# HGRN scores of levels 0 to 5: four products of 32 keys per block of 128 tokens instead of one of 128 keys

## The reference

```
q, fp, i_in, gate = split(h @ w_in, 4)
f = lb + (1 - lb) * sigmoid(fp);  k = (1 - lb) * sigmoid(-fp)
scores[t, s] = sum_k q[t, k] * k[s, k] * exp(bcum[t, k] - bcum[s, k])   for s <= t
o[t] = sum_s scores[t, s] * v[s] + (q[t] * exp(bcum[t])) @ S
S_t = diag(f_t) S_{t-1} + k_t v_t^T
```

## Time and profile before

| | us |
|---|---|
| median of 3 runs | 1762.22 |
| lowest and highest | 1761.44, 1766.76 |
| the profiled execution | 1766.25 |
| its span on the core | 1764.4 |
| mean granted TensorE clock | 0.986 |
| PE busy | 1686.6 (96%) |
| DVE busy | 1039.5 (59%) |
| ACT, POOL busy | 555.5 (31%), 382.6 (22%) |

### The profile page before, as it was taken

One profiled execution on the slowest core, in us unless ns is written; L12 is line 12 of the kernel. 1 busy time (PEld: TensorE's weight loads), 2 busy tenths in 40 slices (PEclk: granted clock), 3 DMA queues, 4 the chain that ended last, 5 costly groups with the idle time before them and its releaser, 6 DMA issues.

```text
span 1764.4 us, 27067 instructions
## 1 busy us (share of the span) xinstructions
PE 1686.6 (96%) x10586; PEld 1479.8 (84%) x10586; DVE 1039.5 (59%) x1635; ACT 555.5 (31%) x1000; POOL 382.6 (22%) x345
## 2 busy tenths in 40 slices
PE   7999999999999999999999899988999999989998
PEld 5999999989998899799998788766887887668876
DVE  5757475644765557465574345667444757764445
ACT  4323132333143232324323143544112225351121
POOL 0000000000421124041331304325341043253410
PEclk9999999999999999999999899999999999999999
DMA  3233232213221221212122123222233242212331
GB/s 125 96 93 94 66 97 85 96 48 101 72 61 60 73 70 58 82 56 72 49 73 84 48 75 104 72 72 67 77 103 113 82 140 72 72 48 82 109 119 48
DMA packets 112608, 141.95 MB, mean 80 GB/s; under 512 B 3068, under 2 KB 88480, under 8 KB 112480
## 3 DMA queue, kind: packets, MB, share of 16 engines
q1 hardware_dynamic: 108368, 133.07, 23.8%
q10 hardware_dynamic: 4032, 6.89, 1.2%
q0 software_dynamic: 80, 0.20, 0.0%
HBM read 137.01 MB, written 2.10 MB: 79 GB/s over the span
## 4 chain that ended last, share of the span: by engine, by line
PE 84%; DVE 8%; ACT 5%; issue 2%; DMA 0%; POOL 0%; SPq 0%; DVEq 0%; ACTq 0%; POOLq 0%
PE acc L363 23%; PE acc L365 23%; PE acc L364 22%; PE aux L514 5%; DVE sm L1828 1%; PE aux L363 1%; PE aux L365 1%; PE aux L364 1%; PE aux L531 1%; ACT pr L1373 1%; PE aux L422 1%; PE aux L539 1%; PE aux L541 1%; PE aux L503 1%; PE aux L1053 1%
## 5 line engine op out<-in xcount | busy, mean ns | idle before, releaser
L363 PE MATMUL acc<-xhi,whi 128*128 128x264 f32 (+2 forms) x1888 | 632.1, 335 | 10.5 <-issue 3.7
L364 PE MATMUL acc<-xlo,whi 128*128 128x264 f32 (+2 forms) x1888 | 618.3, 327 | 0.0
L365 PE MATMUL acc<-xhi,wlo 128*128 128x264 f32 (+2 forms) x1888 | 617.9, 327 | 0.0
L363 PEld LDWEIGHTS acc<-xhi,whi 128*128 128x128 f32 x1888 | 357.9, 190 | 46.9 <-issue 12.2
L365 PEld LDWEIGHTS acc<-xhi,wlo 128*128 128x128 f32 x1888 | 358.0, 190 | 30.7
L364 PEld LDWEIGHTS acc<-xlo,whi 128*128 128x128 f32 x1888 | 358.3, 190 | 27.5
L358 POOL TENSOR_TENSOR wlo<-raw,whi 128x1024 fp32r<-128x1024 f32 x84 | 205.0, 2441 | 352.5 <-DVE whi L1883 352.5
L354 ACT ACTIVATE whi<-raw 128x1024 fp32r<-128x1024 f32 x160 | 165.8, 1048 | 173.1 <-PE acc L365 157.7
L1676 DVE TENSOR_TENSOR wlo<-raw,whi 128x1024 fp32r<-128x1024 f32 x77 | 93.9, 1222 | 69.1 <-ACT whi L354 69.1
L358 DVE TENSOR_TENSOR wlo<-raw,whi 128x1024 fp32r<-128x1024 f32 x83 | 101.0, 1221 | 42.5 <-ACT whi L354 42.5
L1883 DVE CAST whi<-raw 128x1024 fp32r<-128x1024 f32 x84 | 65.7, 784 | 73.0 <-PE acc L365 73.0
(11 more groups left out here) (281 smaller groups left out, 2733.5 us busy)
## 6 DMA issues: line engine op xcount, KB each, us to landing
raw<-in_w_in SPq DMA_DIRECT2D x38, 1024.0 KB, 5.1
raw<-in_hgrn_w_in SPq DMA_DIRECT2D x32, 1024.0 KB, 5.8
raw<-in_pool_w_in SPq DMA_DIRECT2D x16, 1024.0 KB, 5.5
raw<-in_pool_w_out SPq DMA_DIRECT2D x8, 1024.0 KB, 4.9
raw<-in_hgrn_w_out SPq DMA_DIRECT2D x8, 1024.0 KB, 4.9
raw<-in_w_out SPq DMA_DIRECT2D x8, 1024.0 KB, 4.9
raw<-in_pool_w_grp SPq DMA_DIRECT2D x4, 1024.0 KB, 5.5
raw<-in_w_branch_attn SPq DMA_DIRECT2D x4, 1024.0 KB, 4.9
```

Of the source, the lines that this page charges most:

```text
L363: pe.matmul(dst, stat[0], mov[0], start=first, stop=False)
L364: pe.matmul(dst, stat[0], mov[1], start=False, stop=False)
L365: return pe.matmul(dst, stat[1], mov[0], start=False, stop=last)
```

## The change

At levels 0 to 5 each block of 128 tokens gets four products of 32 keys on the diagonal: keys 32n to 32n + 31 by the same 32 tokens' queries (level 0), or by their 16 queries in second halves (levels 1 to 5), written to partitions 32n to 32n + 31. The masked copies are the same and read all 128 partitions; what is off the diagonal is masked away there, and `aux` is set to zero once, on DVE, ahead of the HGRN stage.

```
-                    for c in range(CH if level <= MASKED else 0):
-                        keys = kb[par][x][:, META + P * c:META + P * c + P]
-                        q = qb[par][x][:, P * c:P * c + P]
+                    for c, n in [(c, n) for c in range(CH) for n in range(4)] if level <= MASKED else []:
+                        rows = slice(32 * n, 32 * n + 32)
+                        keys = kb[par][x][:, META + P * c + 32 * n:META + P * c + 32 * n + 32]
+                        q = qb[par][x][:, P * c + 32 * n:P * c + 32 * n + 32]
                         if level == 0:
-                            dst = small[:, P * c:P * c + P]
+                            dst = small[rows, P * c + 32 * n:P * c + 32 * n + 32]
                         else:
                             q = second_halves(q, m)
-                            dst = small[:, 64 * c:64 * c + 64].rearrange("p (b m) -> p b m", m=m)
+                            dst = small[rows, 64 * c + 16 * n:64 * c + 16 * n + 16]
+                            dst = dst.rearrange("p (b m) -> p b m", m=m)
                         mm = pe.matmul(dst, keys, q, start=True, stop=True)
...
             weighted_inverse(dve, 1)
+            dve.memset(aux[:, :, :], 0.0)
```

## The result

| | us |
|---|---|
| the kernel before, median of 4 runs | 1761.83 (1760.91 to 1766.76) |
| the changed kernel, median of 4 runs | 1732.44 (1731.22 to 1733.81) |
| ratio | 0.9828, 95% interval 0.9808 to 0.9848 |
| the changed kernel, profiled execution | 1731.74, span 1729.9 |

The change makes the kernel 29.4 us faster. 1728.5 was forecast, in a range of 1719 to 1748.

A forecast was written before the change was run, and what follows sets the result against it. PE was taken to bound the kernel; 41.8 us from cheaper steps, less 7.0 of waiting for DVE and 1.1 of memset, gave 33.7 us, so 1728.5 us against the median of 1762.22, range 1719 to 1748.

The forecast's parts named there:

- PE bounds the stage: HGRN stage: PE is busy for 96% of the span, so every us it saves counts until another engine is late.
- the step cost 1.79 us before: One level of both heads on PE, levels 0 to 5: 1.79 us each, 48 steps, 86 us.
- A changed step costs what level 6 costs: Levels 0 to 5 on PE: 0.84 us written out, 1.00 in the loop, four bands overlapping; gain 41.8 us.
- the straight line: PE's time per record extrapolated from 128 keys (107 ns) and 64 keys (67 ns): 47 ns at 32 keys.
- slower: Rival: neighbouring bands don't overlap, each small record takes 47 ns; 62 us more, 1825 us; chance 0.04.
- two readings: Level steps: four bands overlap, or rival, they give no more than two: 16.7 us gain, 1745.5 us, chance 0.22.
- The memset has no cover: Zeroing `aux` on DVE ahead of PE's third HGRN unit: its whole length goes onto PE, 1.1 us.
- What is late next: PE waits for DVE's level work at levels 2 and 3: 1.0 us a pair in 7 pairs, 7.0 us given back.
- POOL at nothing: POOL's level work, 3.46 us in its densest window, was costed at nothing.
- The sum 41.8 - 7.0 - 1.1 = 33.7: Whole kernel: PE's gain from cheaper steps, less waiting for DVE, less the memset, in us.
- DVE takes more: Rival: DVE's stretch of levels 1 to 4 sets the pace, 2.2 us a pair; 25.3 us gain, 1737; chance 0.12.

The follow-up runs named there:

- the one, two and four bands: Changed kernel with all products written to one band or two bands, against its own four: steps of 2.016, 1.009 and 0.554 us first to last start.
- e1: Changed kernel with DVE's queue reordered: factors of the pair to come and weight split placed behind level work; 1721.61 us, ratio to before 0.9751.
- e2: Changed kernel with level 1 alone put back to one product of 128 keys by 64 queries per block; 1732.41 us.

## Why the prediction was right, and which term was off

- **PE bounds the stage, and the step cost 1.79 us before.** Right: 91.5 us over 42 steps include what the unit itself takes between the same records.
- **A changed step costs what level 6 costs, since a band gets as many records.** Right, and shown by the one, two and four bands. Nearly free of waits (kernel e1) the 42 steps gained 91.5 - 55.6 = 35.9 us; the forecast for them was 24 x 0.79 + 18 x 0.95 = 36.1. The steps in the loop gained 0.80 us each, the others 0.92. Pair 7 gained 5.5, the forecast was 5.7. One price beside it was off: by the straight line a record of 32 keys on one band took 47 ns, and the rival "slower" was reckoned with that; it takes 32. The mechanism is what I read from two bands; that neighbours don't share a path was my choice between two readings, with 0.22 for the other, and no row before could tell.
- **The memset has no cover.** Right: 0.91 us of record, 0.9 us of wait, 1.1 forecast.
- **What is late next.** The engine, the cause and the first place were right (level 2, for the masked copies of L581, now L584), the size was not: this is the term that was mis-sized. I took 1.0 us a pair, 7.0; it is 64.4 - 55.6 = 8.8, and 9.7 us, 1.4 a pair, with the 0.9 at level 6, which no forecast wait covers. Its split was off as well: I had 0.6 us at level 2 and 0.3 to 0.5 at level 3, and it is 8.0 of the 8.8 us at level 2, 1.1 a pair, and 0.7 at level 3, 0.1 a pair. At level 2 I had reckoned with one wait; there are two, since each head waits for its own copy (0.46 and 0.44 us in the rows shown; over the pairs the stretch of level 2 grew from 2.25 to between 2.40 and 2.74 us, where kernel e1 has 1.33 to 1.42). I had also let DVE's rows keep their length and start, but they start with the unit's end and the two rows of factors grew from 0.55 + 1.11 to 1.00 + 0.86 us. POOL's work of level 1 starts at 442.47 now and runs beside the first of them (442.63), where it ran beside the second before (445.54 and 445.74). It is what I suspect for the growth; no run tested it.
- **What I had no row for.** In pairs 0 and 2 the last of level 6's 32 records starts 0.50 and 0.47 us behind the one before it, which is the 0.9 us of level 6; the 31 ahead of it, the second head's too, come at their usual pace:

```profile
461.86 0.74 PE L503 MATMUL aux<-qb,kb 128*32 128x32 f32 x31
462.90 0.19 PE L503 MATMUL aux<-qb,kb 128*32 128x32 f32 x1 [0.30 <-issue]
```

The profile names no engine for it. It is gone in e1 and e2, but also nearly gone in the kernel with the moved memset (0.2 us in pair 0, nothing in pair 2), whose steps wait for DVE as those of the changed kernel do. So the cause stays open.
- **POOL at nothing.** It cost nothing directly: no row of PE's waits names POOL in this stretch. Whether it lengthens DVE's rows is open, as said above.

The sum 41.8 - 7.0 - 1.1 = 33.7 should have read 41.4 - 9.7 - 0.9 = 30.8. My alternative "DVE takes more" named the right engine as well, at 2.2 us a pair, and the measured time lies half way between the two. But it made DVE's load set the pace, and kernel e1 shows that the load did not.

## What to carry to other kernels

Where products of 32 keys and at most 32 queries follow each other, write neighbours in the code to different bands of 32 partitions: what counts is how many records the fullest band gets, not how many there are. Before making the bounding engine's step cheaper, look at the engine whose result that step waits for: not only how busy it is between two steps, but what stands in its queue ahead of the result. An order that costs the steps nothing now can be worth nearly a third of the gain once the other engine is faster (8.8 of 29.4 us), and it is free to change.

## What the runs showed that I had not expected

- The order by band: the same 64 records on the same four bands take 0.554 us when the bands alternate and 1.316 when four products in a row go to one band.
- A fully busy engine need not hold anyone up: DVE is busy for 4.10 of 4.10 us in e1's window, and PE for 4.02; the view of waits names none in a step of this kernel.
- Undoing a sixth of the change costs nothing that can be measured: 1732.41 against 1732.44 us.
- The other order of DVE's queue gained 2.9 us between the steps in both kernels' profiles, before the change and after it.
